# The V side of an expert mixer moved from sixteen rows behind the U side to twenty-four

## What is computed

```python
def peer(h, wq, keys, u_tab, v_tab):          # blocks of 128 tokens
    def one_block(xb):
        q = (xb @ wq).reshape(n, 8, 2, 128)
        s = jnp.einsum('nhpd,hpkd->nhpk', q, keys)
        sv, si = lax.top_k(s, 16)
        cand = sv[:, :, 0, :, None] + sv[:, :, 1, None, :]
        fv, fi = lax.top_k(cand.reshape(n, 8, 256), 16)
        eidx = ...                                    # expert numbers of the 16 best
        gate = jax.nn.softmax(fv, axis=-1)
        ue = jnp.take(u_tab, eidx, axis=0)
        act = jax.nn.gelu(jnp.einsum('nhkd,nd->nhk', ue, xb))
        ve = jnp.take(v_tab, eidx, axis=0)
        return jnp.einsum('nhk,nhkd->nd', gate * act, ve)

for l in range(2):
    x = x + m2 * mixer(modulate(x, m0, m1))   # even_mixer or odd_mixer
    x = x + m5 * peer(modulate(x, m3, m4))
y = rms_norm(x, final_norm_g)
```

## Time and profile before

| | |
|---|---|
| runs | 4653.35 us median, 4649.7 to 4653.51 |
| profiled execution | 4650.03 us, its span 4648.2 us |
| PE, PE weight loads | 48%, 23% busy |
| DVE | 59% busy |
| ACT | 23% busy |
| POOL | 52% busy |
| bytes moved | 1583.75 MB, 1342.34 MB of them the U and V gathers |
| mean rate | 341 GB/s |

### The profile page before, as it was taken

How to read it: one execution, slowest core, us unless ns; L and a number is a source line. 1 busy time by engine, 2 the same in 40 slices (tenths; PEclk the granted TensorE clock), 3 DMA queues, 4 the chain that set the end, 5 groups by cost and what they waited for, 6 DMA issues and landing times.

```text
span 4648.2 us, 39716 instructions
## 1 busy us (share of the span) xinstructions
PE 2217.2 (48%) x11298; PEld 1061.8 (23%) x11298; DVE 2721.4 (59%) x6959; ACT 1065.9 (23%) x3545; POOL 2436.7 (52%) x2564
## 2 busy tenths in 40 slices
PE   4548565565933433333454378635753332233233
PEld 4444343234511200000341034403420000000000
DVE  1454755775355566666446655376556675666764
ACT  1131232222211112212122222222322221212211
POOL 0023434543265467677346743366357666677675
PEclk7779767667966755565675689867875566556566
DMA  5586778777699999999899997899999999999998
GB/s 184 179 297 238 277 256 308 290 275 270 240 363 384 384 381 403 402 394 399 289 380 394 404 351 275 315 401 389 352 346 400 364 399 370 369 391 398 384 398 335
DMA packets 578410, 1583.75 MB, mean 341 GB/s; under 512 B 50058, under 2 KB 237930, under 8 KB 578066
## 3 DMA queue, kind: packets, MB, share of 16 engines
q0 software_dynamic: 368640, 1342.34, 74.9%
q1 hardware_dynamic: 186514, 217.94, 14.0%
q10 hardware_dynamic: 23040, 20.98, 1.3%
HBM read 1554.62 MB, written 26.44 MB: 340 GB/s over the span
## 4 chain that ended last, share of the span: by engine, by line
PE 25%; DMA 22%; DVE 21%; POOL 12%; issue 12%; ACT 7%; SPq 1%; DVEq 0%; POOLq 0%; ACTq 0%
PE ps_box L925 10%; DMA u_ring<-in_peer_u_dram,idx 10%; POOL v_ring L815 6%; PE ps_v L870 6%; POOL u_ring L805 6%; DVE u_ring L1590 4%; DMA w_slots<-in_w_mod_dram 4%; ACT w_v L1224 4%; DMA v_ring<-in_peer_v_dram,idx_v 3%; PE ps_box L1083 3%; DVE HT L1807 2%; ACT idx_v L1234 1%; DVE onehot L1606 1%; DMA w_slots<-in_peer_keys_dram 1%; PE ps_v L896 1%
## 5 line engine op out<-in xcount | busy, mean ns | idle before, releaser
L1590 DVE CUSTOM_DVE_ANT_0 u_ring<-u_ring,h_cur 128x1024 f32<-128x1024 f32 x1280 | 1534.2, 1218 | 916.2 <-DMA u_ring<-in_peer_u_dram,idx 905.9
L815 POOL DMA_INDIRECT v_ring<-in_peer_v_dram,idx_v x1280 | 1216.0, 950 | 1381.2 <-PE ps_v L870 834.0
L870 PE MATMUL ps_v<-v_ring,w_diag 128*32 128x512 f32 x5120 | 1014.1, 933 | 1657.5 <-DMA v_ring<-in_peer_v_dram,idx_v 1008.7
L805 POOL DMA_INDIRECT u_ring<-in_peer_u_dram,idx x1280 | 1220.5, 954 | 811.2 <-issue 343.7
L870 PEld LDWEIGHTS ps_v<-v_ring,w_diag 128*32 128x32 f32 x5120 | 194.4, 147 | 2390.2 <-issue 1596.5
L925 PE MATMUL ps_box<-HT,w_slots 128*128 128x128 f32 (+2 forms) x1792 | 477.9, 429 | 80.3 <-ACT AR L1444 31.7
L1241 ACT ACT_TABLE_LOAD x79 | 101.4, 1283 | 1164.2 <-DVE act_v L1590 1155.1
L925 PEld LDWEIGHTS ps_box<-HT,w_slots 128*128 128x128 f32 x1792 | 295.5, 210 | 265.0 <-issue 152.7
L1224 ACT ACTIVATE w_v<-w_tok 32x4 f32<-32x4 f32 x1280 | 265.7, 208 | 193.4 <-DVE w_tok L1649 179.4
L1234 ACT ACTIVATE idx_v<-idx 32x4 uint32<-32x4 uint32 x1280 | 265.9, 208 | 16.3 <-ACT AR L1455 0.4
L1083 PE MATMUL ps_box<-w_slots,CAT 128*128 128x256 f32 x640 | 153.2, 402 | 26.2 <-ACT CAT L1429 9.4
(11 more groups left out here) (163 smaller groups left out, 2252.9 us busy)
## 6 DMA issues: line engine op xcount, KB each, us to landing
w_slots<-in_w_mod_dram SPq DMA_DIRECT2D x48, 1024.0 KB, 7.9
w_slots<-in_peer_wq_dram SPq DMA_DIRECT2D x48, 1024.0 KB, 13.0
u_ring<-in_peer_u_dram,idx POOLq DMA_INDIRECT x1280, 7.1
v_ring<-in_peer_v_dram,idx_v POOLq DMA_INDIRECT x1280, 7.2
w_slots<-in_w_in_odd_dram SPq DMA_DIRECT2D x16, 1024.0 KB, 15.0
w_slots<-in_w_in_even_dram SPq DMA_DIRECT2D x14, 1024.0 KB, 7.9
BC<-modrow SPq DMA_DIRECT2D x26, 512.0 KB, 7.3
w_slots<-in_w_out_even_dram SPq DMA_DIRECT2D x12, 1024.0 KB, 11.7
```

The costliest lines, as they stand in the source:

```text
L805: pool.indirect_dma_start(out=u_ring[:, k % NU, :], out_offset=None, in_=u_rows, in_offset=bass.IndirectOffsetOnAxis(ap=idx[:, h % 2, k:k ...
L815: pool.indirect_dma_start(out=v_ring[:, k % NV, :], out_offset=None, in_=v_rows, in_offset=bass.IndirectOffsetOnAxis(ap=idx_v[:, h % 2, k: ...
L870: last = nc.tensor.matmul(ps_v[QUARTER * q:QUARTER * q + QUARTER, 512 * half:512 * half + 512], w_diag[:, c % GROUPS, q, :], v_ring[:, (r ...
L1590: nc.vector.tensor_tensor_reduce(u_ring[:, k % NU, :], u_ring[:, k % NU, :], h_cur[:, :], 1.0, 0.0, ALU.mult, ALU.add, act_v[:, h % 2, k:k ...
```

## The change

V goes from 16 to 24 rows behind U. The constants and the positions in the orders change, no arithmetic does:

- POOL gathers with U row k of head i the V row k+8 of head i-2 where k is under 8, and V row k-8 of head i-1 from there on. PE multiplies the four groups of head i-1 at rows 11 and 15 of head i and rows 3 and 7 of head i+1, and DVE writes their diagonals after dots 10, 13, 0 and 4.
- `weigh` goes from the end of row 15, behind `topk`, to row 6 of the next head. `seg_end` goes from row 15 to row 24 of a segment.
- On ACT `gelu`, `exps` and `load_s` go from row 15 to row 4 of the next head (`exps` and `load_s` then name the same heads' successors one head later), `spread_weights` from row 0 to row 8 and `spread_indices` from row 0 to row 12. `take_h`, which copies the next segment's vectors into `h_cur`, stays at row 127 and gets a wait for the dots.
- The mixers beside segments 2, 4 and 6 start after 26, 26 and 28 rows (before: 16, 16 and 20), that beside segment 5 after 28 (before: 24).
- At the end 24 V rows stand behind the last U row, before 16. The waits' bases in the loops' registers follow.

```diff
-DIAG_AT = (2, 4, 8, 12)
+V_LAG = 8
+LATE = 4
+WEIGH = 6
+DIAG_AT = (10, 13, 0, 4)
...
-         (1, SMP): {"start": 8, "norm": 1, "f": 2, "f_end": 4, "cv": 4, "cv_end": 4, "Y": 1, "ff": 1, "out": (1, 2),
+         (1, SMP): {"start": 12, "norm": 1, "f": 2, "f_end": 4, "cv": 4, "cv_end": 4, "Y": 1, "ff": 1, "out": (1, 2),
...
 def behind(seg, r):
 
-    if r >= TOPK:
-        return seg, r - TOPK
+    if r >= TOPK + V_LAG:
+        return seg, r - TOPK - V_LAG
     if isinstance(seg, int) and seg == 0:
         return None
-    return seg - 1, r + ROWS - TOPK
+    return seg - 1, r + ROWS - TOPK - V_LAG
...
                 for k in range(TOPK):
                     gather_u(i, h, k)
-                    if not first:
-                        gather_v(i - 1, h - 1, k)
+                    if k < V_LAG and not first and not (isinstance(i, int) and i == 1):
+                        gather_v(i - 2, h - 2, k + V_LAG)
+                    elif k >= V_LAG and not first:
+                        gather_v(i - 1, h - 1, k - V_LAG)
...
+            for k in range(V_LAG, TOPK):
+                gather_v(78, 6, k)
             for k in range(TOPK):
                 gather_v(79, 7, k)
...
             start(2)
-            rows(TOPK)
+            rows(TOPK + V_LAG + 2)
             cond(1)
...
-            def gelu(seg, h):
-                i = seg * 8 + h
+            def gelu(i, h):
                 wait(act, w_done, i - 1, "gelu")
                 wait(act, dots_done, 16 * i + 16)
                 nc.scalar.activation(gelu_v[:, h % 2, :], act_v[:, h % 2, :], ACT.Gelu_apprx_tanh).then_inc(gelu_done, 1)
 
-            def exps(seg, h):
-
-                i = seg * 8 + h
+            def exps(i, h):
+
                 wait(act, negmax_done, i + 1)
                 wait(act, w_done, i - 3, "exps")
                 nc.scalar.activation(ex[:, h % 4, :], fv[:, h % 2, :], ACT.Exp, bias=neg_max[:, h % 2:h % 2 + 1],
...
             def take_h(seg):
 
+                wait(act, dots_done, 128 * seg, "h")
                 wait(act, h_landed, 16 * seg + 16)
...
                     place[1] += 1
-                    if r % TOPK == 0:
-                        i = seg * 8 + r // TOPK
+                    i, h = seg * 8 + r // TOPK, r // TOPK
+                    if r % TOPK == LATE and not (isinstance(i, int) and i == 0):
+                        late(seg, i, h)
+                    if r % TOPK == V_LAG:
                         if not (isinstance(i, int) and i == 0):
                             spread_weights(i - 1)
-                        spread_indices(i, r // TOPK)
-                    if r % TOPK != TOPK - 1:
-                        continue
-                    h = r // TOPK
-                    last = isinstance(seg, int) and seg == 9
-                    gelu(seg, h)
-                    if h == 0 and (seg if isinstance(seg, int) else seg.loop.lo) >= 6:
-                        seg_square(seg - 1)
-                    if h == 7 and not last:
+                        if h == 1 and (seg if isinstance(seg, int) else seg.loop.lo) >= 6:
+                            seg_square(seg - 1)
+                    if r % TOPK == 12:
+                        spread_indices(i, h)
+                    if r == ROWS - 1 and not (isinstance(seg, int) and seg == 9):
                         take_h(seg + 1)
-                    if h < 6 or not last:
-                        exps(seg + (h + 2) // 8, (h + 2) % 8)
-                    if h < 5 or not last:
-                        load_s(seg + (h + 3) // 8, (h + 3) % 8)
+
+            def late(seg, i, h):
+                last = isinstance(seg, int) and seg == 9
+                gelu(i - 1, h - 1)
+                if h < 7 or not last:
+                    exps(i + 1, h + 1)
+                if h < 6 or not last:
+                    load_s(i + 2, h + 2)
 
             def start(seg):
...
             start(9)
             rows(ROWS)
+            gelu(79, 7)
             spread_weights(79)
             seg_square(9)
...
                     dot(seg, r)
-                    if r % TOPK in DIAG_AT and behind(seg, r) is not None:
-                        diagonal(seg * 8 + r // TOPK - 1, DIAG_AT.index(r % TOPK))
-                    if r % TOPK != TOPK - 1:
-                        continue
-                    h = r // TOPK
-                    static = isinstance(seg, int)
-                    if h == 0 and not (static and seg == 0):
+                    i, h, static = seg * 8 + r // TOPK, r // TOPK, isinstance(seg, int)
+                    if r % TOPK == WEIGH and not (static and i == 0):
+                        weigh(i - 1, h - 1)
+                    if r % TOPK in DIAG_AT:
+                        c = DIAG_AT.index(r % TOPK)
+                        of = i - 1 if c < 2 else i - 2
+                        if not (static and of < 0):
+                            diagonal(of, c)
+                    if r == TOPK + V_LAG and not (static and seg == 0):
                         seg_end(seg - 1, int(seg > 5) if static else seg.loop.lo // 5)
-                    if h < 6 or not (static and seg == 9):
+                    if r % TOPK == TOPK - 1 and (h < 6 or not (static and seg == 9)):
                         topk(seg + (h + 2) // 8, (h + 2) % 8)
-                    weigh(seg, h)
...
             rows(ROWS)
+            for c in range(2, GROUPS):
+                diagonal(78, c)
+            weigh(79, 7)
             for c in range(GROUPS):
                 diagonal(79, c)
```

44 lines of the change are left out of this document (21 added, 23 removed).

## The result

The changed kernel takes 4605.82 us (median of 4 runs, 4601.33 to 4609.72) beside 4651.52 for the kernel before on the same chip: a ratio of 0.9902, 95% interval 0.9885 to 0.9919. It is 46 us faster, where 154 were forecast.

A forecast was written before the change was run, and what follows sets the result against it. Full DMA bounds expert-only stretches, handovers between in-order engines those beside segments 0 and 1's mixers. -45 - 44 - 100 + 10 + 11 + 14 = -154 us from 4650 gives 4496, said as 4500; 8-in-10 range 4400 to 4640.

The forecast's parts named there:

- (a): Rival: only the rings gain; beside mixers PE and the mixer's handovers bound; 4570 to 4600 us, 24% together with (d).
- (d): Rival: the DMA is full already, so terms except beside the mixers are near 0 or losses; 4585 us, 24% with (a).
- signs of being wrong: DVE waiting for GELU at `weigh`, ACT's spreads still ahead of PE's needs, or segment 5's mixer start costing 30 us.
- Beside the mixers: About 28 heads beside mixers or modulation rows: spreads no longer delay attention's exponentials, 7.2 us each, half taken: -100 us.
- The ninth gather: At a head's end outside the mixers, POOL's 2.4 us wait for PE goes; 2.5% of 1800 us: -45 us.
- Segment ends: `seg_end` moved away from `topk`, its pause mostly covered by the rings; three ends 8 us each, five about 4: -44 us.
- Later diagonals: In projections, PE waits longer for diagonals behind a mixer's instruction, on a third of mixer heads: +10 us.
- The mixer beside segment 5: Fewer rows between `seg_end` and the mixer's start leave about 10 us more of waiting for new tokens: +11 us.
- The tail: After the last dot PE has seven groups to do instead of five: +14 us.
- (b): Rival: ACT and PE overlap with all of `topk`, 10 us or more per mixer head; under 4450 us, 16%.
- (c): Rival: DVE stops at `weigh` for a late GELU, a new wait making the kernel slower; 4 us a head give 4710, 11%.

The follow-up runs named there:

- tlag: Changed kernel with GELU, `weigh` and the weights' spread back at the head's end, V still 24 rows behind, indices' spread left at row 12: 4604.8 us.
- wfirst_d0: Kernel before with `weigh` ahead of `topk`, the weights' spread right behind GELU, and a head's first diagonal at row 0 instead of 2: 4589.8 us.
- wfirst: Kernel before with `weigh` ahead of `seg_end` and `topk` and the weights' spread right behind GELU, diagonals unmoved: 4671.1 us.
- segend: Kernel before with `seg_end` two dots behind `topk` and mixers beside segments 2 and 4 starting two rows later: 4668.9 us.
- segend20: Kernel before with `seg_end` five dots behind `topk` and mixers beside segments 2, 4 and 6 starting later: 4655.8 us.
- tlag_d8: `tlag` with diagonals at rows 8, 12, 0 and 4 instead of 10, 13, 0 and 4: 4601.6 us.
- tlag_d7: `tlag` with diagonals at rows 7, 11, 15 and 3 instead of 10, 13, 0 and 4: 4600.9 us.
- start9: Changed kernel with the mixer beside segment 5 started three rows earlier, at row 25 instead of 28: 4576.3 us.
- wmid_d0: `wfirst_d0` with `weigh` inside `topk`, behind its first two sorts: 4568.4 us.
- wmid_d0_m: `wmid_d0` with one head's weights and the next head's indices spread together, in 16 copies of 32 x 8 plus two plain copies: 4526.9 us.

## Why the prediction was right and wrong

**Direction and range held**, the predicted time did not: 4606 us lies in the outer range of 4400 to 4640, in the part given to cases (a) and (d), and not in the forecast's own range of 4450 to 4560. Of the 154 us that were forecast 46 came. Two of the signs of being wrong that it names came true: ACT's spreads still stand ahead of what PE waits for, and segment 5 cost 31 us rather than 11.

**Beside the mixers (-100 us, the step that failed).** Segments 0 and 1 gave 40 us; segments 2, 4 and 6 gave 4 together. The term took 7.2 us in each of 28 heads, 202 us, and half of that. (Its 28 heads and the 42 or so that 1800 us outside the mixers hold leave ten of the 80 heads uncounted, and of the chain's 232 us in both spreads 67 lie in segments 3, 7, 8 and 9, not about 90; neither changes the verdict.) The mechanism was real, a spread directly ahead of an exponential of the attention, but both of its factors were too large. Leaving the spreads out altogether wins 99 us and not 202, and 81 of them lie in the 16 heads of segments 0 and 1: beside segments 2, 4 and 5 the spreads cost next to nothing. And of these 81 us the change takes only half: two attention heads stand between the experts' exponentials and the first spread, but the spreads, taken apart, still stand ahead of exponentials, and 42 us stay. That ACT could serve the attention while DVE is in `topk`, because GELU and `weigh` stand later, gave nothing: `tlag`, which has them back at the head's end, takes 562.6 and 523.9 us in segments 0 and 1, 38 less than before.

**The ninth gather (-45 us).** The heads 59 to 63 and 66 to 71 fell from 216.0 to 210.7 and from 258.7 to 253.6 us, but 74 to 78 rose from 210.2 to 211.2, although the gather behind `topk` goes out 5.6 us after it as reckoned. On 42 heads outside the mixers that is some -25. The forecast let all of the wait go because it kept POOL's arrival at that gather where it was, at 4454.28; but POOL waits at other groups now. Added up from the traces, POOL's waits beyond the usual 0.3 us were 3.2 us a head in segments 7 and 8, all at the ninth gather, and are 2.1 and 2.3 now, of which 1.4 and 1.5 at the ninth; in segment 9 they were 2.1 and are 2.3. That is the change of the heads' times within 0.1 us. My estimate from this is that POOL sets the pace there: 16 pairs of gathers at 2.49 us are 39.8 us, and with the waits 43.0 before and 41.9 now in heads 59 to 63, which take 43.2 and 42.1. `wfirst_d0` bears it out: against `wfirst`, POOL's waits in these heads fall by 1.4 us and the heads by 1.5. A head of segment 7 before (the gather goes out 0.8 us after PE's last product has ended, though the profile names a dot), then one after:

```profile
3783.71 3.64 PE L870 MATMUL ps_v<-v_ring,w_diag 128*32 128x512 f32 x16 [10.17 <-DVE w_diag L1599]
...
3788.16 0.93 POOL L815 DMA_INDIRECT v_ring<-in_peer_v_dram,idx_v  x1 [3.31 <-DVE act_v L1590]
```

```profile
3752.87 0.94 POOL L818 DMA_INDIRECT v_ring<-in_peer_v_dram,idx_v  x1 [1.69 <-DVE act_v L1598]
```

The Trainium skill's limit of about 358 GB/s for loads from HBM ("DMA: Bandwidth & Descriptors", section "Where 436 GB/s comes from") would have allowed no gain in these heads; the stretches now stand at 404 and 406 GB/s, and the measurement decides.

**Segment ends (-44 us).** Right in mechanism and, for the three in layer 1, in size: some 25 us against 24. `segend` and `segend20` show that a part of it comes from the dots between the two pauses alone. The other five ends, -20 us in the forecast, lie beside mixers or the modulation rows and can't be read apart from them.

**Later diagonals (+10 us).** Not there: PE waited 647.5 us for diagonals before and waits 355.5 now, and `tlag_d8` and `tlag_d7` move them ahead for no gain.

**The mixer beside segment 5 (+11 us, measured +31).** The wait at its start rose by 16.2 us; the 10 us counted about four rows fewer between `seg_end` and the mixer, and left out that `topk` had stood between them too. But `start9`, with a wait as long, takes 31 us less in segment 5, so the wait alone does not explain the loss; its cause stays open.

**The tail (+14 us).** Right: from the last dot to the end it is 41.3 us before and 54.7 after, 13.3 more (15.6 from the start of the last head).

**Rivals.** (a) is the case that came nearest, for another reason than it gave: PE's projections do not bound segments 0 and 1, since without spreads they are 81 us shorter. (b), overlap with all of `topk`, did not come at all. (c), DVE held at `weigh` by a late GELU, did not come either: 51.7 us in 7 places against 63.2 before. Another wait for ACT grew, that of the diagonals for their weights (90.5 us in 9 places); `tlag`, where it is 3.2 us, takes the same time, so it costs nothing. (d) is half true: with V 24 rows behind, 406 GB/s is reached, and no variant tried here moved those heads any more; but with V 16 rows behind `wmid_d0` reaches 409 and takes 206.7 us for heads 74 to 78, so the DMA was not what held them at 42 us.

## What to carry to other kernels

A chain of handovers may be covered link by link: here three dots hid the spread and the spread hid three dots; moving the one lost 22 us, moving the other won 17, and moving both won 59. A share of the chain of waits is not a price: 232 us on the chain were worth 99. Before moving work of an in-order engine away from a crowded place, look at what stands ahead of what in the new place, and price the work itself by leaving it out. When an order shifts against a mixer or any other stream of loads, try its start a few rows to either side: three rows earlier were worth 22 to 32 us here, three rows later nothing clear.

## What the runs showed of the hardware

- Two pauses of DVE, of 10 and 11 us where they adjoin, cost 4 us less in three places together with two dots between them, 9 less with five, and some 25 less with nine, where the second pause is 8 us and V stands 24 rows behind.
- Loads issued among gathers land late: the short convolution's weights needed 18.6 us (kernel before, 2674.31 to 2692.93) and 21.3 us (after, 2643.05 to 2664.33), and the last three of eight weight tiles cost PE 1.4, 11.2 or 23.5 us of waiting by the row at which the mixer started.
- POOL's gathers follow one another every 1.24 us when nothing holds them. In the kernel before, a gather that waited for PE goes out 0.3 us after PE's product has ended in segment 9 (4456.68 to 4456.98), and 0.8 us after it in segments 2, 3, 7 and 8, which POOL runs in loops (3787.35 to 3788.16). After the change 0.8 is also seen in some places outside the loops; why, no run shows.
- One core held 409 GB/s with a DMA share of 1.03 over 207 us. The stretch is the last heads of `wmid_d0_m`:

```profile
4234.00:4441.00 207.00, 71.60 (x320) 13.16 (x320) 144.51 (x375) 34.67 (x115) 151.20 (x161) 0.58 1.03 409
```

- A copy of 32 x 8 values takes ACT hardly longer (215 ns, on the page of `wmid_d0_m`) than one of 32 x 4 (208 ns in the mean of 1280, on the page of the kernel before):

```profile
L1246 ACT ACTIVATE wi_v<-w_tok 32x8 f32<-32x8 f32 x1264 | 271.3, 215 | 220.5 <-issue 139.2
```
